# Thirty-two of the 384 dense tokens take their first expert layer from rows fetched head by head

## What is computed

```python
def block(xt):
    q = (xt @ w_query).reshape(PEER_BLOCK, PEER_HEADS, D_QUERY)      # 8 heads
    s1 = jnp.einsum("thc,nc->thn", q[..., :half], k1)                # 128 keys each
    s2 = jnp.einsum("thc,nc->thn", q[..., half:], k2)
    v1, i1 = lax.top_k(s1, PEER_TOPK)                                # 16
    v2, i2 = lax.top_k(s2, PEER_TOPK)
    ...
    top, pos = lax.top_k(cand, PEER_TOPK)                            # 16 of the 256 sums
    eidx = jnp.take_along_axis(cidx, pos, axis=-1)                   # i1 * 128 + i2
    g = jax.nn.softmax(top, axis=-1)
    hid = jnp.einsum("thkd,td->thk", u_tab[eidx], xt)                # first layer
    a = g * jax.nn.gelu(hid, approximate=False)
    return jnp.einsum("thk,thkd->td", a, v_tab[eidx])                # second layer
```

## Time and profile before

| | |
|---|---|
| median of 3 runs | 1707.75 us (1703.96 to 1707.88) |
| the profiled execution | 1703.0 us, its span 1701.4 us |
| TensorE busy | 1622.1 us, 95% |
| VectorE busy | 1353.9 us, 80% |
| ScalarE busy | 777.5 us, 46% |
| POOL busy | 613.5 us, 36% |
| moved by DMA | 463.54 MB, mean 272 GB/s |
| largest groups on TensorE | first layer, 3 x 1024 matmuls of 384 columns; second layer, 3 x 768 of 512 columns |

### The profile page before, as it was taken

The page is one execution under the profiler, slowest core; times in us unless marked ns, Lnnn a source line. Parts: engine busy times, 40 slices in busy tenths (PEclk is TensorE's granted clock), DMA queues, the critical chain, the costliest instruction groups (busy, mean ns, idle before and its releaser), DMA issues.

```text
span 1701.4 us, 27754 instructions
## 1 busy us (share of the span) xinstructions
PE 1622.1 (95%) x9666; PEld 1460.0 (86%) x9666; DVE 1353.9 (80%) x3162; ACT 777.5 (46%) x1273; POOL 613.5 (36%) x538
## 2 busy tenths in 40 slices
PE   5999988798999999989999999999999999999997
PEld 4999744497999999989999999997888888888886
DVE  4324585353799999979999999987999999999996
ACT  4222373233434433367777767753333333333334
POOL 0000380054444444654334334432343333433320
PEclk9999997997999999999999999999999999999999
DMA  3342562722343333499999999999999999999991
GB/s 119 106 164 92 167 190 91 264 89 77 114 148 109 122 114 109 156 364 375 384 372 393 387 367 393 400 405 388 404 403 399 404 404 399 405 403 399 402 366 53
DMA packets 158621, 463.54 MB, mean 272 GB/s; under 512 B 18224, under 2 KB 64432, under 8 KB 154546
## 3 DMA queue, kind: packets, MB, share of 16 engines
q1 hardware_dynamic: 98930, 248.59, 39.7%
q0 software_dynamic: 50944, 178.96, 27.6%
q10 hardware_dynamic: 8640, 34.61, 5.1%
HBM read 406.12 MB, written 57.63 MB: 273 GB/s over the span
## 4 chain that ended last, share of the span: by engine, by line
PE 60%; DVE 13%; POOL 3%; DMA 2%; issue 1%; ACT 1%; another core or an unknown queue 0%; SPq 0%; ACTq 0%; POOLq 0%
PE va L230 10%; PE va L232 10%; PE va L231 10%; PE hp L230 6%; PE hp L231 6%; PE hp L232 6%; DVE gathered L1511 3%; DVE og L2039 3%; DVE ulo L2050 3%; PE ggp L1979 2%; DVE vw L1511 2%; PE qzp L230 2%; PE qzp L232 2%; PE qzp L231 2%; PE qsp L1680 1%
## 5 line engine op out<-in xcount | busy, mean ns | idle before, releaser
L230 PE MATMUL hp<-mid_hi,uhi 128*128 128x384 f32 x1024 | 354.0, 346 | 9.9 <-DVE ulo L2050 3.6
L231 PE MATMUL hp<-mid_lo,uhi 128*128 128x384 f32 x1024 | 344.8, 337 | 0.0
L232 PE MATMUL hp<-mid_hi,ulo 128*128 128x384 f32 x1024 | 343.5, 335 | 0.0
L230 PE MATMUL va<-vhi,ahi 128*128 128x512 f32 x768 | 299.8, 390 | 2.8 <-DVE hid L1511 2.1
L232 PE MATMUL va<-vhi,alo 128*128 128x512 f32 x768 | 299.5, 390 | 0.0
L231 PE MATMUL va<-vlo,ahi 128*128 128x512 f32 x768 | 299.3, 390 | 0.0
L1909 POOL DMA_INDIRECT gathered<-in_v_experts,eidx x160 | 175.6, 1098 | 310.3 <-DVE acc L2359 221.5
L230 PEld LDWEIGHTS hp<-mid_hi,uhi 128*128 128x128 f32 x1024 | 192.9, 188 | 15.0 <-DVE ulo L2050 5.8
L232 PEld LDWEIGHTS hp<-mid_hi,ulo 128*128 128x128 f32 x1024 | 193.0, 188 | 0.0
L231 PEld LDWEIGHTS hp<-mid_lo,uhi 128*128 128x128 f32 x1024 | 192.8, 188 | 0.0
L1420 ACT ACTIVATE uhi<-uw 128x1024 fp32r<-128x1024 f32 x126 | 132.8, 1054 | 116.1 <-PE hp L232 114.6
(11 more groups left out here) (328 smaller groups left out, 3448.6 us busy)
## 6 DMA issues: line engine op xcount, KB each, us to landing
uw<-in_u_experts SPq DMA_DIRECT2D x128, 512.0 KB
vw<-in_v_experts SPq DMA_DIRECT2D x68, 512.0 KB
more_v<-in_v_experts SPq DMA_DIRECT2D x60, 512.0 KB
gate_matrix<-gst ACTq DMA_DIRECT2D x12, 2048.0 KB
hidden_values<-gelu_out SPq DMA_DIRECT2D x72, 192.0 KB
hd_mid<-hidden_values SPq DMA_DIRECT2D x8, 1536.0 KB
gt_mid<-gate_matrix SPq DMA_DIRECT2D x8, 1536.0 KB
hd_freed<-hidden_values SPq DMA_DIRECT2D x7, 1536.0 KB
```

The costliest lines, as they stand in the source:

```text
L230: nc.tensor.matmul(out, a_hi, b_hi, start=first, stop=False)
L231: nc.tensor.matmul(out, a_hi, b_lo, start=False, stop=False)
L232: return nc.tensor.matmul(out, a_lo, b_hi, start=False, stop=last)
```

## The change

The last 32 dense tokens (`OWN`; the tokens on partitions 96 to 127 of token tile 3) take their first layer from fetched rows; called *own* tokens here, and their products *own dots*. The first-layer matmuls and their GELU are then 352 columns wide (`DENSE`). The other parts:

- For head j, VectorE computes the 32 x 16 expert numbers of the own tokens (`own_stage`). SP spreads them with four small DMAs over four groups of 32 partitions (`own_spread`), so that four indirect fetches of 128 rows (`own_fetch`, on POOL) bring all 512 rows. VectorE makes four own dots (`own_dot`) behind steps 10, 12, 14 and 16 of the chain of head j + 1, against a copy of the tokens' inputs in PSUM (`x2own`).
- `own_fetch` of heads 0 to 5 stands at the head of POOL's turns 2 to 7. That of head 6 stands ahead of POOL's subtraction for e2, that of head 7 behind the one for e9. The subtractions for e10 and e11 go to VectorE (`LENT`), with the last four own dots between and behind them.
- ScalarE applies GELU to the 32 own values per partition, SP brings them back to the tokens' partitions, and VectorE multiplies them into the gates `GG` before `table_prep` 3. The stored hidden values of the own tokens are 1.0 (`ge[:, :, DENSE:]`), so the second layer is as wide as before.
- Nine row fetches are requested before the gate stage (`EARLY`) where it was four; three dots are made before `table_prep` 3 and fifteen before the turns, and the turns have 22, 21, 22, 21, 22 and 22 dots.
- The loops over the heads are written out on all engines.

```diff
+OWN = 32
+DENSE = TD - OWN
...
-                last = mm3(hp[i][:, :TD], uhi[:, i, k], ulo[:, i, k], x2hi[:, k, P:SEQ], x2lo[:, k, P:SEQ],
+                last = mm3(hp[i][:, :DENSE], uhi[:, i, k], ulo[:, i, k], x2hi[:, k, P:P + DENSE], x2lo[:, k, P:P + DENSE],
...
+        LENT = 10
+        EARLY = (5, 7, 8, 9, 9, 9)
+        OWN_LINKS = (10, 12, 14, 16)
+        FIRST_DOTS, BEFORE_TABLE, BEFORE_TURNS = 15, 3, 9
+        TURN_DOTS = (22, 21, 22, 21, 22, 22)
...
+            def own_spread(sp, j):
+                sp.wait_ge(own["picked"], j + 1)
+                if j:
+                    sp.wait_ge(own["dot"], j * OWN_SLOTS)
+                for g in range(OWN_GROUPS):
+                    sp.dma_start(own_index[g * OWN:(g + 1) * OWN, :], own_stage[mine, g * OWN_SLOTS:(g + 1) * OWN_SLOTS]).then_inc(own["index"], 16)
+
+            def own_fetch(pool, j):
+                pool.wait_ge(own["index"], 16 * OWN_GROUPS * (j + 1))
+                if j:
+                    pool.wait_ge(own["dot"], j * OWN_SLOTS)
+                else:
+                    pool.wait_ge(own["copied"], 1)
+                for n in range(OWN_SLOTS):
+                    settle(pool)
+                    nc.gpsimd.indirect_dma_start(own_buffers[n], None, u_table,
+                                                 bass.IndirectOffsetOnAxis(ap=own_index[:, n:n + 1], axis=0)).then_inc(own["row"], 16)
+
+            def own_dot(dve, j, n):
+                dve.wait_ge(own["row"], 16 * OWN_SLOTS * (j + 1))
+                nc.vector.tensor_tensor_reduce(out=own_buffers[n], in0=own_buffers[n], in1=x2own[:], scale=1.0, scalar=0.0,
+                                               op0=ALU.mult, op1=ALU.add, accum_out=own_hid[:, j, n:n + 1]).then_inc(own["dot"], 1)
...
-                with sp.Fori(0, NH - 1) as j:
+                for j in range(NH - 1):
...
+                    if j:
+                        own_spread(sp, j - 1)
+                for e in range(QX + UR):
                     u_fetch(sp, RT * NH + e, e % UR)
...
+                    if e == UR - 1:
+                        own_spread(sp, NH - 2)
+                    if e == LENT:
+                        own_spread(sp, NH - 1)
...
+                    if e == QX:
+                        sp.wait_ge(own["act"], 1)
+                        for g in range(OWN_GROUPS):
+                            sp.dma_start(own_act[mine, :, g * OWN_SLOTS:(g + 1) * OWN_SLOTS], own_hid[g * OWN:(g + 1) * OWN]).then_inc(own["back"], 16)
...
                 def turn(j, last):
 
+                    if j >= 2:
+                        own_fetch(pool, j - 2)
...
-                for e in range(QX - 1):
-                    u_split_lo(pool, RT * NH + e + 2, e % 2, (e + 2) % UR)
-                    if e == QX - 3:
-                        for n in range(SG):
-                            request(pool, n)
+                for j in range(NH):
+                    turn(j, j == NH - 1)
+                own_fetch(pool, NH - 2)
+                for e in range(2, LENT):
+                    u_split_lo(pool, RT * NH + e, e % 2, e % UR)
+                own_fetch(pool, NH - 1)
+                for n in range(EARLY[0]):
+                    request(pool, n)
+                pool.wait_ge(u_lo, RT * NH + LENT + 1 + 3)
+                for i, e in enumerate(range(LENT + 2, QX + 1)):
+                    u_split_lo(pool, RT * NH + e, e % 2, e % UR)
+                    for n in range(EARLY[i], EARLY[i + 1]):
+                        request(pool, n)
...
+                        if j and links[0] in own_at:
+                            own_dot(dve, j - 1, own_at[links[0]])
                         dve.wait_ge(qs["chain"], j * LINKS + links[0])
...
+                nc.vector.scalar_tensor_tensor(own_stage[mine], pk[mine, 0, :, OWN_TILE], float(NK), pk[mine, 1, :, OWN_TILE],
+                                                   ALU.mult, ALU.add).then_inc(own["picked"], 1)
...
+                dve.wait_ge(u_lo, RT * NH + LENT - 1 + 3)
+                for u in range(2):
+                    split_lo(dve, RT * NH + LENT + u, (LENT + u) % 2, (LENT + u) % UR)
+                    for n in range(u * OWN_SLOTS // 2, (u + 1) * OWN_SLOTS // 2):
+                        own_dot(dve, NH - 1, n)
...
+                dve.wait_ge(own["back"], 16 * OWN_GROUPS)
+                nc.vector.tensor_tensor(GG[mine, OWN_TILE], GG[mine, OWN_TILE], own_act[mine].rearrange("p h k -> p (h k)"), ALU.mult).then_inc(table_prep, 1)
```

137 lines of the change are left out of this document (82 added, 55 removed).

## The result

The changed kernel takes **1767.5 us** (median of four runs, 1763.3 to 1769.2) where the kernel before took 1705.9 in the same runs: 1.0363 times as long, interval 1.0330 to 1.0397. The forecast was 1722, range 1694 to 1744. The sign is right, the size isn't: the loss is 62 us instead of 14, and the result lies outside the range. The profiled execution has a span of 1765.4 us, 64.0 more than before.

A forecast was written before the change was run, and what follows sets the result against it. VectorE was taken to set routing's pace; TensorE, VectorE and DMA were all full in the gate turns. Terms +30.5 - 13.9 - 1.7 - 0.5 = +14.4 on 1703.0 gave 1717.4, plus 4.75 to the median: 1722 us, range 1694 to 1744.

The forecast's parts named there:

- e11: Twelfth of the sixteen tiles, counted from 0, behind routing: starts 51 us behind the start of VectorE's head 7.
- A matmul step of 352 columns, 160 ns: First-layer products on TensorE: a 352-column matmul starts every 160.0 ns, 13.6 ns less, 0.33 us per tile.
- I take 2.6 us: VectorE's later routing heads: standstills beside POOL's subtractions cost 2.6 us per head, 6 us in the first heads.
- the standstills stay: Rival, routing on VectorE: heads of 39.4 us, head 7 at 703, gate stage at 779, 1738 us; chance 0.18.
- S + 10.6: Start of the third of the sixteen tiles, 10.6 us behind the start of VectorE's head 7, at 699 us.
- can't be made up: TensorE's 20 us stop ahead of the third of the sixteen tiles is lost, since VectorE's chain now leads.
- by 47.5 (2.5 us is an estimate): Head 7's own rows land 47.5 us behind that head's start on VectorE, with fetches issued by 45.
- From there to the gate stage, 23.7 us: From e11 to the gate stage: five tiles 19.2 us, POOL's subtractions about 3.5, transposes 1.
- e14: Fifteenth of the sixteen tiles, counted from 0, behind routing: the own tokens' gates, ready near S + 62, hide behind it.
- The first turn, 69 us: First gate turn: 69 us instead of 70.7, -1.7 us, its third tile's wait staying.
- Later turns, 61.9 us: Last five gate turns: 61.9 us each, where VectorE and DMA agree; 309.5 instead of 323.4, -13.9 us.
- The last eight tiles, -0.5: Last eight tiles, where fetches and loads end the waits: -0.5 us, between 0 and -2.6.

The follow-up runs named there:

- unrolled: The kernel before with only the loops over the heads written out on all five engines: 1.0038, 1710.2 us.
- wide: The changed kernel without the own tokens' path and with 384 columns, nothing left out: 1.0112 against the kernel before, 1724.0 us.
- no_own: The changed kernel without the own tokens' path (indices, fetches, dots, GELU, way back): 1.0073 against the kernel before, 1715.7 us.
- no_dots: The changed kernel with the own dots left out, every index and fetch kept: 1.0206 against the kernel before, 1738.0 us.
- width_alone: The kernel before with first-layer products 352 columns wide and nothing else: 1.0005.
- no_fetch: The changed kernel without own indices and fetches; own dots multiply rows loaded once: 1.0239 against the kernel before, 1745.5 us.
- late_e2: The changed kernel with head 6's own rows fetched in two pairs behind later POOL subtractions of the sixteen tiles: 1.0365 against the kernel before.
- order_back: The changed kernel with late_e2's edit and the waits for the end of VectorE's chain put back in four queues: 1.0326 against the kernel before.
- no_own_order_back: order_back without the own tokens' path: 1.0083 against the kernel before, 1716.4 us.
- no_own_lent_back: no_own with the two subtractions lent to VectorE back on GpSimd, its first row requests behind the last tile's subtraction: 1.0138 against the kernel before.
- dots_first: The kernel before with three of its first five dots moved ahead of the subtraction of the gate stage's second tile: 1.0005.

## Why the forecast was right in sign and wrong in size

By the ratios, and 1704 us for the kernel before, the 62 us are made up of: written-out loops 6 (unrolled), new order and new dealing of the dots 13 (wide less unrolled), narrower products -7 (no_own less wide), the own path without its dots 23 (no_dots less no_own), the own dots 27 (changed less no_dots). Each of these differences is uncertain by 3 to 7 us; that they add up to 62 is by construction. In the kernel before, the narrower products bring nothing (width_alone): what a part is worth depends on the others.

The forecast's sum against the profiled execution was 1717.4; that execution took 1766.9. The 49.5 us between them, by its own steps:

- **A matmul step of 352 columns, 160 ns: right.** In a tile at 880 us ten steps take 1.60 us.

```profile
880.20 0.32 PE L236 MATMUL hp<-mid_lo,uhi 128*128 128x352 f32 x1
...
881.80 0.32 PE L237 MATMUL hp<-mid_hi,ulo 128*128 128x352 f32 x1
```

- **One head, "I take 2.6 us" of standstills: the step that failed first.** Own dots were right (3.9 us per head against 4.0), and so was it to follow VectorE. But the standstills did not move away. My argument was that GpSimd, once it starts a turn only behind the head two before, meets steps that don't collide; at 515 us it starts such a turn with a backlog, does its work without gaps, and holds up the cast. That is only a part of it: without one own fetch heads 1 to 7 still take 39.7 us (no_fetch), 3.8 more than without own dots (no_own), so the dots come on top of standstills that stay, and own fetches add 0.9 per head. Heads 1 to 7 came to 40.6 us, beyond the 39.4 that I had as the bound. By my own sum (30 + 3.9 - 0.4) that leaves about 7 us per head where I had put 6 in the first and 2.6 in the later ones. Head 7 started at 709.2 instead of 688.8, **+20.4** (head 0 +1.5, head 1 +2.0, head 2 +6.8, heads 3 to 6 together +9.7, the start +0.3), and took 43.2 instead of 35.5, **+7.7**. The rival "the standstills stay" had this outcome for the heads, and 0.18; its reason, GpSimd's added fetches, is worth 6 us of A.
- **e2 at S + 10.6: right** (720.2 - 709.2 = 11.0), **and "can't be made up" wrong.** late_e2 shows that the stop costs nothing by itself. It did no harm to the sum, since the sum followed the chain, but it named the wrong culprit. The 3 us for the lower clock were right: from e2 to the next tile it is 6.6 us (720.22 to 726.84) instead of 3.84.
- **Own rows of head 7 landed "by 47.5 (2.5 us is an estimate)": wrong.** The last issue ends at 761.5 and the first dot starts at 769.58, 8.1 us later. From the chain's end to e11 it took 20.7 us instead of 15.5, **+5.2**. The timelines of GpSimd and VectorE:

```profile
756.79 0.95 POOL L1594 DMA_INDIRECT vw<-in_u_rows,own_index  x1 [5.41 <-DMA own_index<-own_stage]
...
760.54 0.94 POOL L1594 DMA_INDIRECT vw<-in_u_rows,own_index  x1 [0.30 <-issue]
```

```profile
769.58 1.22 DVE L1599 CUSTOM_DVE_ANT_0 vw<-vw,x2own 128x1024 f32<-128x1024 f32 x1 [14.04 <-DMA vw<-in_u_rows,own_index]
...
789.04 0.29 DVE L1916 TENSOR_TENSOR GG<-GG,own_act 32x128 f32<-32x128 f32 x1 [5.29 <-DMA own_act<-own_hid]
```

- **From there to the gate stage, 23.7 us: right in size** (24.3, **+0.6**), in part by luck: e11 took 6.6 us (773.14 to 779.69) at the lower clock, which the sum didn't have here. And the own gates are ready at 789.0, as e14 starts, where "near S + 62" is 771; VectorE waited 5.3 us for them.
- **The first turn, 69 us: wrong, +8.5.** It takes 77.5, and 75.2 without any own token, so this is the price of the new order and dealing. I had counted the dots, not the waits: VectorE waits 12 us in B before, 22 in no_own, 31 now. The third tile is an example: its stop is 9.19 us instead of 3.55 (which the forecast reads as 3.9 from the earlier trace rows). VectorE's subtraction for it runs from 816.70 to 817.91, and of the six dots ahead of it two wait, 2.06 us for rows and 1.44 for nothing that the profile names.
- **Later turns, 61.9 us: VectorE's busy time was right, the length wrong, +6.8.** VectorE's busy time is 61.7 us per turn (308.7 / 5), as forecast. But a turn is that plus what VectorE waits: 1.4 us before (323.4 - 316.3 over five) and 1.5 now. I had put a turn equal to the busy time of one engine, although the kernel before shows 63.3 busy and 64.7 long. Of the gain of 14 that the forecast booked here 7 came.
- **The last eight tiles, -0.5: nothing came**, +0.4.

These make 49.6.

The range was too narrow for the same reason: its upper end joined the standstills' rival with turns of 62.6 us, but took neither the first turn nor the landing of the own rows beyond a single value.

What stays open: what of the 6 us of the written-out loops is code loading and what is order wasn't tried. Nor is it settled why B of no_own is 20 us longer than before: order_back's edits bring 6 of them (and A is 5 longer), the written-out loops have 4, the new dealing (fifteen dots ahead of the turns instead of five) should be most of the rest, which is argued from VectorE's 10 us more of work in B (84.0 against 73.7) and its 17.0 us of waits for rows (none before), not shown by a run of its own. And what VectorE's steps lose to GpSimd's subtractions was never measured by taking these away; it is read from steps beside them.

## What to carry to other kernels

Where TensorE and VectorE are each busy 98% of a loop or more and the transfers fill it too, shortening one brings next to nothing (width_alone: 2 us of 323), and the floors have to be measured one at a time: cut the work of one engine far beyond what you mean to do and see where the loop stops. Before you move work onto an engine, ask whether that engine, not the busiest one, sets the pace of the stretch: here VectorE did, and 28 dots of 1.235 us went 27 us into its chain. And a long stop in the profile is not a cost until a run without it is faster; this one moved, twice.

## What I had not expected of the hardware

- A cast of 0.40 us took 8.88 us: VectorE got no turn between the second and the last of five subtractions of GpSimd that followed one another without a gap.
- That 16 to 18 us more of such standing still in the casts went with only 6 us of A (no_dots and no_own, changed and no_fetch). It looks as if the collisions were a nearly constant tax of GpSimd's 51 to 57 subtractions, wherever in the head they fall; that is argued, not shown. Six more of them in A went with 9 us more of VectorE's busy time (order_back), five more with 5 (no_own_order_back), but two more with 4 less (no_own_lent_back).
- Rows fetched by GpSimd land late: 8.1 us behind the last issue of four, with four more fetches and a few loads issued meanwhile; 6.6 us from the first issue to the first dot in dots_first, which waited for them.
- TensorE's granted clock is 0.90 over 402 to 797 us (0.99 before). It falls to 0.5, the lower level of 1.2 GHz, within the stops and comes back some us after their end. That is so in routing too, where TensorE now waits for VectorE ahead of key scores (stops of 11.7, 5.4, 8.1 and 6.9 us; low from 555.5 for 13.7 us, from 599.8 for 6.8, from 637.4 and from 678.4 for 10.2 each), then at e2 (20.5 us from 705.7), at e11 (13.7 from 763.7) and in the first turn (10.2 from 811.5).
- TensorE is busy 325.4 us over 402 to 797 us instead of 324.9 over 402 to 733, in about as many matmuls (2098 and 2086 rows), although its products are narrower. Narrower products should give 48 x 0.33 = 16 us there. TensorE is busy 34.8 us of the low stretches, 7.7 before, and half of the difference is 14 us (an estimate), so the lower clock took back most of it.
